# RWKV chunk inversion, levels 1 to 5: products over 64 rows and 32 columns of the block-diagonal operands

## The reference

```python
def step(s, inp):
    r_t, w_t, k_t, v_t, kk_t, a_t = inp
    sa = jnp.einsum('bhvk,bhk->bhv', s, -kk_t)
    s = s * w_t[:, :, None, :] + sa[..., None] * (kk_t * a_t)[:, :, None, :] + v_t[..., None] * k_t[:, :, None, :]
    return s, (jnp.einsum('bhvk,bhk->bhv', s, r_t) if with_output else None)

s, ys = lax.scan(step, s0, seq, reverse=reverse)
```

## Time and profile before

| | us |
|---|---|
| median of 3 runs | 5543.41 |
| lowest, highest | 5526.74, 5548.75 |
| profiled execution | 5546.16 |
| its span in the trace | 5544.5 |
| mean granted clock of PE | 0.902 |

### The profile page before, as it was taken

How to read it: one execution, slowest core, us unless ns; L and a number is a source line. 1 busy time by engine, 2 the same in 40 slices (tenths; PEclk the granted TensorE clock), 3 DMA queues, 4 the chain that set the end, 5 groups by cost and what they waited for, 6 DMA issues and landing times. The chain is left out here.

```text
span 5544.5 us, 89787 instructions
## 1 busy us (share of the span) xinstructions
PE 4587.4 (83%) x38202; PEld 3517.5 (63%) x38202; DVE 2619.6 (47%) x4076; ACT 1615.9 (29%) x2683; POOL 498.8 (9%) x483
## 2 busy tenths in 40 slices
PE   6999878888885877956888577777999999787999
PEld 4888667777774555732222354446888878576787
DVE  4556566766664763530000325554444222376553
ACT  3222223322222553320000313333223121464322
POOL 0000010110100653000000001210000000000000
PEclk8999989899996898978999887778999999898999
DMA  6656700000001103318999220002122223212232
GB/s 231 224 190 226 249 28 13 13 13 13 17 5 49 33 33 132 105 47 329 422 422 373 101 72 16 16 16 95 58 65 63 71 91 118 90 58 72 84 100 94
DMA packets 169377, 616.47 MB, mean 111 GB/s; under 512 B 24176, under 2 KB 37488, under 8 KB 143664
## 3 DMA queue, kind: packets, MB, share of 16 engines
q1 hardware_dynamic: 155136, 548.22, 27.7%
q0 software_dynamic: 13872, 62.92, 2.9%
HBM read 533.32 MB, written 77.75 MB: 110 GB/s over the span
## 5 line engine op out<-in xcount | busy, mean ns | idle before, releaser
L1745 PE MATMUL f_acc<-f_a_lo,f_w_hi 128*128 128x512 f32 x4048 | 1037.4, 359 | 65.0 <-DVE f_a_lo L1967 29.9
L1745 PEld LDWEIGHTS f_acc<-f_a_lo,f_w_hi 128*128 128x128 f32 x4048 | 668.3, 190 | 187.0 <-issue 43.9
L1745 PE MATMUL f_acc<-f_a_lo,f_w_lo 128*128 128x512 f32 x2288 | 687.9, 356 | 0.0
L1734 DVE TENSOR_TENSOR f_w_lo<-f_w_raw,f_w_hi 128x1024 fp32r<-128x1024 f32 (+1 forms) x176 | 228.3, 1298 | 538.8 <-ACT f_w_hi L1729 538.8
L1745 PEld LDWEIGHTS f_acc<-f_a_lo,f_w_lo 128*128 128x128 f32 x2288 | 379.4, 190 | 66.0
L1729 ACT CAST f_w_hi<-f_w_raw 128x1024 fp32r<-128x1024 f32 (+1 forms) x176 | 194.7, 1107 | 613.7 <-DMA f_w_raw<-in_ffn_w_up 219.9
L1745 PE MATMUL i_acc<-i_x_hi,i_w_hi 128*128 128x512 f32 (+1 forms) x1024 | 307.4, 356 | 16.3 <-DVE i_x_lo L2500 11.9
L335 DVE COPY_PREDICATED rw_work<-rw_mask_x,rw_big 128x512 f32<-128x512 uint8 x288 | 238.3, 879 | 157.1 <-PE rw_big L626 151.9
L1745 PE MATMUL i_acc<-i_x_hi,i_w_lo 128*128 128x512 f32 (+1 forms) x1024 | 309.6, 358 | 0.0
L1745 PE MATMUL i_acc<-i_x_lo,i_w_hi 128*128 128x512 f32 (+1 forms) x1024 | 305.9, 355 | 0.0
L1389 PE MATMUL ex_big<-ex_w,ex_xe_now 128*64 128x512 f32 x1024 | 237.3, 618 | 75.5 <-DMA ex_w<-in_exp_w 75.5
(11 more groups left out here) (522 smaller groups left out, 8389.4 us busy)
## 6 DMA issues: line engine op xcount, KB each, us to landing
ex_w<-in_exp_w SPq DMA_DIRECT2D x192, 1024.0 KB, 17.5
i_mod_rows<-in_ada_rows SPq DMA_DIRECT2D x128, 512.0 KB, 4.9
f_w_raw<-in_ffn_w_up SPq DMA_DIRECT2D x88, 512.0 KB, 3.5
i_w_raw<-in_w_in_both SPq DMA_DIRECT2D x44, 512.0 KB, 3.8
f_w_raw<-in_ffn_w_down SPq DMA_DIRECT2D x32, 704.0 KB, 4.0
i_w_raw<-in_w_in_lat SPq DMA_DIRECT2D x40, 512.0 KB, 4.6
pt<-i_stage POOLq DMA_DIRECT2D x22, 768.0 KB, 5.8
f_w_raw<-in_hgrn_w_both SPq DMA_DIRECT2D x24, 512.0 KB, 3.6
```

The costliest lines, as they stand in the source:

```text
L1734: dve.tensor_tensor(self.view(self.w_lo, u), self.view(self.w_raw, u), self.view(self.w_hi, u).bitcast(F32), ALU.subtract).then_inc(self.r ...
L1745: op = pe.matmul(acc[:, a:b], part[:, k], xs[:, k0 + k, a:b], start=(first and k == 0 and part is w_hi and xs is x_hi), stop=(last and k = ...
```

## The change

In levels 1 to 5 a product reads only the 64 rows in which its block lies (`work_half`, `t1_half`, and `mg` with rows m to m + 63), picks 32 instead of 64 columns (`split_half`), and writes a quarter of each matrix's region: partitions m to m + 63 and columns q + m / 2 to q + m / 2 + 31 (`in_quarter`). `right` makes its products in the same order as before, so PE's program has as many products as before and in the same order; other engines' instructions are the same but for one memset of 128 x 2 x 128 elements, which clears the part of the banks 4 and 5 (`XT_BANK`) that would otherwise be read before anything is written there. Levels 0 and 6, the masked copies, the T copies and all waits stay.

```diff
@@ -114,6 +114,17 @@
         def t1_ap(buf, off, dims):
             return bass.AP(halves, buf * 8 * CH + off, [[H_F, P]] + dims)
 
+        def split_half(lv):
+            w = 1 << lv
+            blocks = [[2 * w, 32 // w]] if w < 32 else []
+            return blocks + ([[1, w]] if w > 1 else [])
+
+        def work_half(m, off, dims):
+            return bass.AP(work, m * W_F + off, [[W_F, 64]] + dims)
+
+        def t1_half(m, buf, off, dims):
+            return bass.AP(halves, m * H_F + buf * 8 * CH + off, [[H_F, 64]] + dims)
+
         def bank(n):
             return big[:, n]
 
@@ -211,6 +222,7 @@
             @block.vector
             def _(dve):
                 def edges_shift():
+                    dve.memset(big[:, 4:6, 3 * CH:], 0.0)
                     dve.wait_ge(const_in, 16 * 6)
                     e = edge[:].rearrange("p (n m) -> p n m", m=2)
                     dve.tensor_tensor(edge_col[:, 0:3], e[:, 0:3, 0], e[:, 0:3, 1], ALU.add)
@@ -591,6 +603,10 @@
                     part = big[m[0]:m[1], b, q:q + 64]
                     return part if lv in (0, 6) else part.rearrange("p (x w) -> p x w", w=1 << lv)
 
+                def in_quarter(b, q, m, lv):
+                    part = big[m:m + 64, b, q + m // 2:q + m // 2 + 32]
+                    return part if lv == 5 else part.rearrange("p (x w) -> p x w", w=1 << lv)
+
                 def left(i, n):
                     lv, u = UNITS[n]
                     if n == 0:
@@ -602,9 +618,14 @@
                         pe.wait_ge(x_updated, N_UNITS * i + n - 2)
                         pe.wait_ge(t_copied, 18 * i + n - 4)
                     for d, c, h, q in matrices(u):
+                        x_at = xs_at + ((d * 6 + c) * 2 + h) * CH + (d << lv)
                         for m in HALF:
-                            last = pe.matmul(in_halves(T_BANK[n % 2], q, m, lv), mg[:, slot(BA, d, c, h), m[0]:m[1]],
-                                             work_ap(xs_at + ((d * 6 + c) * 2 + h) * CH + (d << lv), split(lv)), start=True, stop=True)
+                            if 0 < lv < LEVELS - 1:
+                                last = pe.matmul(in_quarter(T_BANK[n % 2], q, m[0], lv), mg[m[0]:m[1], slot(BA, d, c, h), m[0]:m[1]],
+                                                 work_half(m[0], x_at + m[0], split_half(lv)), start=True, stop=True)
+                            else:
+                                last = pe.matmul(in_halves(T_BANK[n % 2], q, m, lv), mg[:, slot(BA, d, c, h), m[0]:m[1]],
+                                                 work_ap(x_at, split(lv)), start=True, stop=True)
                     last.then_inc(t_ready, 1)
 
                 def right(i, n):
@@ -618,13 +639,17 @@
                     for d, c, h, q in matrices(u):
                         t_at = (d * 4 + 2 * (c % 2) + h) * CH
                         x_at = xt_at + ((d * 6 + c) * 2 + h) * CH
+                        for m, _ in HALF:
+                            if lv < LEVELS - 1:
+                                pe.matmul(in_quarter(X_BANK[n % 2], q, m, lv), work_half(m, x_at + m, [[1, 64]]),
+                                          t1_half(m, n % 2, t_at + m + (d << lv), split_half(lv)), start=True, stop=True)
                         for m in HALF:
                             if lv < LEVELS - 1:
-                                pe.matmul(in_halves(X_BANK[n % 2], q, m, lv), work_ap(x_at + m[0], [[1, 64]]),
-                                          t1_ap(n % 2, t_at + (d << lv), split(lv)), start=True, stop=True)
-                        for m in HALF:
-                            last = pe.matmul(in_halves(XT_BANK[n % 2], q, m, lv), t1_ap(n % 2, t_at + m[0], [[1, 64]]),
-                                             work_ap(x_at + ((1 - d) << lv), split(lv)), start=True, stop=True)
+                                last = pe.matmul(in_quarter(XT_BANK[n % 2], q, m[0], lv), t1_half(m[0], n % 2, t_at + m[0], [[1, 64]]),
+                                                 work_half(m[0], x_at + m[0] + ((1 - d) << lv), split_half(lv)), start=True, stop=True)
+                            else:
+                                last = pe.matmul(in_halves(XT_BANK[n % 2], q, m, lv), t1_ap(n % 2, t_at + m[0], [[1, 64]]),
+                                                 work_ap(x_at + ((1 - d) << lv), split(lv)), start=True, stop=True)
                     last.then_inc(xx_ready, 1)
 
                 def values(i, u):
```

## The result

The changed kernel takes 5612.18 us (median of 4 runs, 5574.93 to 5622.69), the kernel before, in the runs beside it, 5537.69 us (4 runs, 5526.74 to 5548.75). The ratio is 1.0122, 95% interval 1.0069 to 1.0175: **slower**, by some 75 us, and outside the range of the prediction (5508 to 5580). The profiled execution has a span of 5621.0 us, against 5544.5 before.

The account below looks back on a forecast made before the run. PE paces the inversion, with its instruction supply (a block per 3.9 us) as the limit: 0.5 us saved a tile, 4 us for eight, from 5544.5 or median 5543.4 to 5540 us; range 5508 to 5580.

Parts of the forecast that it names:

- The pace of PE's unit: Inversion, levels 1 to 5: one `left` plus `right` could fall from 2.80 to 1.4 us if nothing else held it.
- The weight load: PE's products, levels 1 to 5: a 64 x 64 load costs half of a 128 x 64 one.
- Streaming halves with the columns: PE's products, levels 1 to 5: going from 64 to 32 moving columns halves the streaming time.
- Supply of instructions: PE's program in the inversion: 256-instruction blocks every 3.9 us hold a 12 us gain to 0.5 us a tile.
- The halves run side by side in one bank: Levels 1 to 5: both row halves work at once; the rival, taking turns, meant 5543 us, chance 0.06.
- Level 1: First three small-product units of each inversion: held by DVE and POOL, so a faster PE gains nothing there.
- memset: One DVE instruction at the stage's start: under 0.75 us, once, hidden by DVE's wait for the constants.
- switching: Between 128- and 64-row products around levels 1 and 6: 0 to 16 us in all, taken as 0.
- The clock: Rival in the inversion: idle PE drops the clock to 1.2 GHz, 5570 us, worst 5595; chance 0.11.

Follow-up runs that it names:

- e5: Changed kernel with the next tile's ten DVE shift steps behind units 6 to 15 instead of 3 to 12; 5528.99 us, ratio 0.998.
- e12: The kernel of e5 again, in more executions on another call's chip; 5538.90 us, ratio 0.9995.
- e2: Changed kernel, but levels 1 to 5 keep 64 moving columns and read 64 rows; 5543.20 us, ratio 1.0007.
- e1: Changed kernel, but levels 1 to 5 read all 128 rows again and keep 32 moving columns; 5545.69 us, ratio 1.001.
- e8: Changed kernel with 32 instead of 64 stationary columns in `right` of levels 1 to 5, half its outputs left out; 5547.69 us.
- e9: As e8, with 32 stationary columns in `right`, but 64 instead of 32 moving columns in levels 1 to 5; 5562.38 us.
- e3: Changed kernel with `XT` outputs of levels 1 to 5 crossed to the other partition half, the inverse left out; 5572.21 us.
- e4: Changed kernel with `right` of levels 1 to 5 reordered: rows 0 to 63 of all eight matrices first, then rows 64 to 127; 6116.31 us.

## Why the prediction was wrong

Two steps failed. The pace of PE's unit was put at 1.4 us by the weight load, and it stayed at 2.80; that alone would not have moved the time, since the sum held the gain back by the supply anyway. What moved it is the clock, which the sum kept at 1.00 (nothing was put in for its loss): the runs show some 75 us lost to it, and none once the pause of level 1 is gone (e5, e12).

- **The weight load (the step that failed first).** "A 64 x 64 load then costs half of today's 128 x 64 one, so PE could run a unit in 1.4 us", taken from L1646 as the nearest row. It costs the same: the unit is 2.80 us with 64 rows (e2), with 32 columns (e1) and with both. The rule given beside it from the Trainium skill, "TensorE: Matmul & The Clock Gate", LDWEIGHTS, that load time goes by columns and not by rows, is borne out by e2. Two signs in the trace of before were passed over. L1646 is a transposition, one load and one matmul in the trace where a product has two of each, and its loads follow one another singly; it was compared with ordinary products without asking what else differs. And the pace was read as one of single records (29 ns), while the records come in pairs 58 ns apart, which is the time of one side of 64 columns. What made L1646 short is not tested.
- **Streaming halves with the columns**: true of a record with a short stationary side only (e8 against e9). With 64 stationary columns the 32 moving ones are hidden.
- **Supply of instructions, a block of 256 per 3.9 us**: right as a mechanism, by e8 and e3, with some 3.7 us measured. But the changed kernel came to it no more than the kernel before, in a few late issue pauses, since its demand stayed at 256 x 14.6 ns = 3.73 us a block. With the clock kept, the forecast of no change would have come true by luck, for a reason other than the one given.
- **The halves run side by side in one bank**: right. e4 shows what turns would look like: 58 ns a record.
- **Level 1, memset, switching, all at nothing**: as predicted; undisturbed inversions take 55.7 to 56.9 us.
- **The clock (the step that made the miss)**: its loss stood in no term of the sum; as a rival it was named, given 0.11 and mis-sized. It let the clock fall because PE would be idle for half of the time; PE was busy for nearly all of it. It took "at 1.2 GHz a block takes about 4.0 us, hardly more than its supply", from the halved work; it takes 256 / 192 x 5.12 = 6.8 us. It priced level 6 and the first solve only, up to 6.5 us a tile; a fall in level 1 costs 27 us a tile, one at level 5 some 5 to 8 against an undisturbed inversion. And it did not ask what the same pause, harmless in the earlier trace rows, does among smaller products. Tile by tile against the kernel before, the long ones cost 27.1, 26.5 and 27.1 us and the late ones 3.6 and 6.7, 91 us; the three undisturbed ones gained 1.3 in sum, so the inversions show some 89. The span grew by 76.5: between the inversions some 7.5 us came back, some 3 ahead of the first and some 3 behind the last.

## What to carry to other kernels

Cutting rows or moving columns of a product that is already small gains nothing while the stationary side stays 64 columns wide: ask which side is the longer and how many quarters of the array work at once. It can lose the clock, though, so look for pauses among such products first, and move what causes them (here ten DVE steps behind a slow POOL) before shrinking anything. Where PE nears one instruction per 14 ns, count instructions: beyond that its program's supply is the limit, and fewer, larger products are what could help.

## What the runs showed of the hardware

- Products of 64x64 in four different quarters run side by side: 64 records in 0.99 us (e3), against 1.87 with two quarters and 58 ns a record with one (e4).
- PE can take an instruction per 8.2 ns for a stretch (e8), but its program comes at 256 per 3.7 us.
- Products of 64 rows and 32 columns did not bring the clock back: 61.4 us at 0.50 with PE busy throughout. It returned at 1097.9, 9.6 us after the first 128-row products of level 6 (1088.3) and 4 us after the last of the small ones (1093.5 to 1093.8).
- At half clock a unit takes 5.12 us, 1.83 times the 2.80, since pairs start 107 ns apart instead of 58.
- Whether a pause of PE loses the clock depends on the products around it: with 64 rows and 32 columns four pauses of 0.63 to 0.67 us in level 1 were each followed by 61.4 us at 0.50, with 64 rows and 64 columns one of 1.46 us was not (e2).
